# Output and down projections with one 512-column matmul over the high and low inputs

## The reference, cut to what matters

```python
def conv_ffn(h, w_in, conv_w, conv_b, w_out):
    z = h @ w_in
    u, g = z[..., :D_FF], z[..., D_FF:]
    a = causal_dwconv(u, conv_w) + conv_b
    return (jax.nn.silu(a) * g) @ w_out

h = h + even_mixer(hn, ...)          # ends in  concat(y_a, y_b) @ w_out
h = h + conv_ffn(rmsnorm(h, g), ...)
h = h + odd_mixer(hn, ...)           # ends in  y @ w_out
```

## Time and profile before

| | us |
|---|---|
| median of 3 runs | 996.73 (994.44 to 996.92) |
| span of the profiled execution | 994.4 (its own time outside the span is not given; the lowest run, 994.44, is the same within 0.1) |
| PE busy | 936.8 (94%) |
| PEld busy | 912.8 (92%) |
| DVE busy | 648.7 (65%) |
| ACT busy | 526.3 (53%) |
| POOL busy | 376.2 (38%) |
| mean granted TensorE clock | 0.976 |

### The profile page before, as it was taken

The page is one execution under the profiler, slowest core; times in us unless marked ns, Lnnn a source line. Parts: engine busy times, 40 slices in busy tenths (PEclk is TensorE's granted clock), DMA queues, the critical chain, the costliest instruction groups (busy, mean ns, idle before and its releaser), DMA issues.

```text
span 994.4 us, 20944 instructions
## 1 busy us (share of the span) xinstructions
PE 936.8 (94%) x7618; PEld 912.8 (92%) x7618; DVE 648.7 (65%) x1109; ACT 526.3 (53%) x847; POOL 376.2 (38%) x158
## 2 busy tenths in 40 slices
PE   8899999994699899999999999989999999999994
PEld 8789999994699899999999999979899999999993
DVE  6998766660454855576666564789747877765366
ACT  6346755550444455575555554545557766664353
POOL 3333434440442432234433433313322444343452
PEclk9899999998799999999999999989999999999997
DMA  7445666572643344456555654334333655565521
GB/s 259 158 148 174 206 201 199 188 232 75 200 166 107 132 151 135 136 173 213 185 172 195 226 184 154 107 127 139 117 121 133 201 188 182 173 228 186 179 80 43
DMA packets 46173, 163.37 MB, mean 164 GB/s; under 512 B 4985, under 2 KB 9593, under 8 KB 46123
## 3 DMA queue, kind: packets, MB, share of 16 engines
q1 hardware_dynamic: 41704, 158.19, 48.7%
q10 hardware_dynamic: 4419, 4.49, 1.3%
HBM read 161.58 MB, written 3.31 MB: 166 GB/s over the span
## 4 chain that ended last, share of the span: by engine, by line
PE 55%; issue 21%; DVE 12%; POOL 5%; ACT 3%; another core or an unknown queue 3%; DMA 1%; SPq 0%; POOLq 0%; ACTq 0%; DVEq 0%
PE psum L1239 17%; PE psum L1240 17%; PE psum L1241 17%; POOL wl L434 5%; DVE work L878 2%; DVE wl L781 1%; DVE h L1214 1%; ACT wh L479 1%; DMA raw<-in_even_in 1%; PE psum L1411 1%; ACT work L640 1%; PE psum L1380 1%; DVE work L1072 1%; PE psum L1388 1%
## 5 line engine op out<-in xcount | busy, mean ns | idle before, releaser
L434 POOL TENSOR_TENSOR wl<-raw,wh 128x1024 fp32r<-128x1024 f32 (+2 forms) x137 | 358.8, 2620 | 581.1 <-ACT wh L479 580.9
L1239 PE MATMUL psum<-xs,wh 128*128 128x256 f32 x1632 | 467.9, 287 | 4.3 <-DVE xs L797 2.1
L1240 PE MATMUL psum<-xs,wh 128*128 128x256 f32 x1632 | 463.2, 284 | 0.0
L1241 PE MATMUL psum<-xs,wl 128*128 128x256 f32 x1632 | 463.1, 284 | 0.0
L479 ACT ACTIVATE wh<-raw 128x1024 fp32r<-128x1024 f32 (+2 forms) x270 | 300.8, 1119 | 286.0 <-PE psum L1241 250.9
L1239 PEld LDWEIGHTS psum<-xs,wh 128*128 128x128 f32 x1632 | 314.5, 193 | 10.9 <-issue 4.0
L1240 PEld LDWEIGHTS psum<-xs,wh 128*128 128x128 f32 x1632 | 314.6, 193 | 0.2
L1241 PEld LDWEIGHTS psum<-xs,wl 128*128 128x128 f32 x1632 | 314.4, 193 | 0.0
L781 DVE TENSOR_TENSOR wl<-raw,wh 128x1024 fp32r<-128x1024 f32 (+1 forms) x133 | 183.8, 1382 | 125.1 <-ACT wh L479 125.0
L1239 PE MATMUL psum<-ys,wh 128*128 128x256 f32 x672 | 192.5, 286 | 22.1 <-DVE h L946 22.1
L1240 PE MATMUL psum<-ys,wh 128*128 128x256 f32 x672 | 191.3, 285 | 0.0
(11 more groups left out here) (195 smaller groups left out, 726.5 us busy)
## 6 DMA issues: line engine op xcount, KB each, us to landing
raw<-in_up SPq DMA_DIRECT2D x132, 512.0 KB, 4.1
raw<-in_down SPq DMA_DIRECT2D x48, 704.0 KB, 4.4
raw<-in_qkv SPq DMA_DIRECT2D x48, 512.0 KB, 3.3
raw<-in_even_in SPq DMA_DIRECT2D x16, 512.0 KB, 4.3
raw<-in_out SPq DMA_DIRECT2D x16, 512.0 KB, 3.4
raw<-in_ple SPq DMA_DIRECT2D x8, 640.0 KB, 3.8
raw<-in_even_out SPq DMA_DIRECT2D x8, 512.0 KB, 3.2
toeplitz_dram<-table_dram ACTq DMA_DIRECT2D x1, 2176.0 KB
```

Source lines behind the costliest of these rows:

```text
L434: nc.gpsimd.tensor_tensor(low, raw[:, s, 0:tiles * P], high.bitcast(f32), ALU.subtract)\
L1239: nc.tensor.matmul(bank, high_w[:, w], high, start=first, stop=False)
L1240: nc.tensor.matmul(bank, high_w[:, w], low, start=False, stop=False)
L1241: done = nc.tensor.matmul(bank, low_w[:, w], high, start=False, stop=last)
```

## The change

For the phases that read `ys`, `unit` gets `halves=True` and a whole bank of 512 columns. High weights meet the high and the low half of the input in one matmul of 512 columns: the first 256 columns of the bank get high by high, the last 256 high by low. Low weights by high input is still a matmul of 256 columns, into the second half. So two matmuls and two weight loads stand for a tile where three stood. The bank's two halves must then be summed: VectorE makes two adds into `h` in place of one (`add_halves`), the second behind a wait for the first (`steps`), and only the second signals `bank_read`. The phases that read `xs` (even_in, up, qkv, ple) stay as they are.

```diff
-        spare_bank = psum[:, 6:7, 0:SEQ]
+        spare_bank = psum[:, 6, :]
...
+            def add_halves(m, bank):
+
+                for half in range(2):
+                    part = bank.rearrange("p (c t) -> p c t", c=2)[:, half:half + 1, :]
+                    added = nc.vector.tensor_tensor(h[:, ds(m, 1), :], h[:, ds(m, 1), :], part, ALU.add)
+                    if half == 0:
+                        steps(added)
+                return added
...
-                        nc.vector.tensor_tensor(h[:, ds(m, 1), :], h[:, ds(m, 1), :], unit_bank(name, i, s), ALU.add)\
-                          .then_inc(bank_read, 1)
+                        add_halves(m, unit_bank(name, i, s)).then_inc(bank_read, 1)
...
-                        nc.vector.tensor_tensor(h[:, ds(m, 1), :], h[:, ds(m, 1), :], proj[:, c:c + 1, 0:SEQ], ALU.add)\
-                          .then_inc(bank_read, 2)
+                        add_halves(m, proj[:, c, :]).then_inc(bank_read, 2)
...
-            def unit(q, s, bank, inputs, tiles, start=True, stop=True, ready=None, read=None):
+            def unit(q, s, bank, inputs, tiles, start=True, stop=True, ready=None, read=None, halves=False):
...
-                    high, low = inputs(t)
                     first, last = start and n == 0, stop and n == len(tiles) - 1
                     w = slice(t * P, (t + 1) * P)
+                    if halves:
+                        nc.tensor.matmul(bank, high_w[:, w], inputs(t), start=first, stop=False)
+                        done = nc.tensor.matmul(bank[:, SEQ:2 * SEQ], low_w[:, w], inputs(t)[:, 0, :], start=False, stop=last)
+                        continue
+                    high, low = inputs(t)
                     nc.tensor.matmul(bank, high_w[:, w], high, start=first, stop=False)
                     nc.tensor.matmul(bank, high_w[:, w], low, start=False, stop=False)
                     done = nc.tensor.matmul(bank, low_w[:, w], high, start=False, stop=last)
...
+            def both_ys(t):
+                return ys[:, t, :, :]
...
             def out_rest(name):
-                each_quad(pe, 1, quads_of[name], quad_of(name, from_ys))
+                each_quad(pe, 1, quads_of[name], quad_of(name, both_ys, whole_bank, True))
...
-                        unit(q, s, slot_bank(c), lambda t: from_ys(b * HALF + t), range(HALF), start=b == 0, stop=b == 1,
-                             ready=ready, read=q * RING - 2 + 2 * c).then_inc(units_done, 1)
+                        unit(q, s, whole_bank(c), lambda t: both_ys(b * HALF + t), range(HALF), start=b == 0, stop=b == 1,
+                             ready=ready, read=q * RING - 2 + 2 * c, halves=True).then_inc(units_done, 1)
```

More of the change, by code:

```diff
@@ L332, in unit_bank @@
                 return spare_bank
-            return proj[:, s:s + 1, 0:SEQ]
+            return proj[:, s, :]
         def column(name, m):
@@ L933, in body @@
                             split_ahead(name, i, s)
-                phase(name, body)
+                phase(name, body, RING)
             def residual_down(name, n):
@@ L955, in body @@
                             split_ahead(name, i, 3)
-                phase(name, body)
+                phase(name, body, 2)
             def up(name, layer, chunks, both):
@@ L1248, in slot_read, with begin, whole_bank @@
                 return None if isinstance(q, int) and q == 0 else q * RING + s - 3
-            def begin(q, slots, bank, read, inputs, ready, late=1):
+            def begin(q, slots, bank, read, inputs, ready, late=1, halves=False):
                 for s in slots:
-                    unit(q, s, bank(s), inputs, range(DC - late), stop=False, ready=ready if s == slots[0] else None, read=read(s))
+                    unit(q, s, bank(s), inputs, range(DC - late), stop=False, ready=ready if s == slots[0] else None, read=read(s),
+                         halves=halves)
                 for s in slots:
-                    unit(q, s, bank(s), inputs, range(DC - late, DC), start=False, ready=ready if s == slots[0] else None)\
-                      .then_inc(units_done, 1)
+                    unit(q, s, bank(s), inputs, range(DC - late, DC), start=False, ready=ready if s == slots[0] else None,
+                         halves=halves).then_inc(units_done, 1)
             def slot_bank(s):
                 return proj[:, s, 0:SEQ]
+            def whole_bank(s):
+                return proj[:, s, :]
             def from_xs(t):
                 return xs[:, t, 0, :], xs[:, t, 1, :]
-            def from_ys(t):
-                return ys[:, t, 0, :], ys[:, t, 1, :]
+            def both_ys(t):
+                return ys[:, t, :, :]
             def statistics(n):
@@ L1273, in statistics, with quad_of @@
                 last.then_inc(stat_ready, 1)
-            def quad_of(name, inputs):
+            def quad_of(name, inputs, bank=slot_bank, halves=False):
                 def quad(i, slots=range(RING)):
@@ L1278, in quad @@
                     for s in slots:
-                        unit(q, s, slot_bank(s), inputs, ALL, read=slot_read(q, s)).then_inc(units_done, 1)
+                        unit(q, s, bank(s), inputs, ALL, read=slot_read(q, s), halves=halves).then_inc(units_done, 1)
                 return quad
@@ L1456, in out_unit @@
                     ready = (lambda t: pe.wait_ge(ys_ready, ys_base[f"att{layer}"] + t + 1)) if s == 0 else None
-                    return unit(out_q, s, unit_bank(out_name, 0, s)[:, 0, :], from_ys, tiles, ready=ready, read=out_q * RING, **flags)
+                    return unit(out_q, s, unit_bank(out_name, 0, s), both_ys, tiles, ready=ready, read=out_q * RING, halves=True, **flags)
                 last_pair = PAIRS - 1
@@ L1529, in _ @@
             q = base["even_out"]
-            begin(q, (0, 1), slot_bank, lambda s: slot_read(q, s), from_ys, lambda t: pe.wait_ge(ys_ready, t + 1), late=2)
-            quad_of("even_out", from_ys)(0, (2, 3))
+            begin(q, (0, 1), whole_bank, lambda s: slot_read(q, s), both_ys, lambda t: pe.wait_ge(ys_ready, t + 1), late=2,
+                  halves=True)
+            quad_of("even_out", both_ys, whole_bank, True)(0, (2, 3))
             out_rest("even_out")
```

## The result

Median of 4 runs 1004.76 us (1004.31 to 1006.37), beside 996.83 (994.44 to 997.97) for the kernel before: ratio 1.0087, 95% interval [1.0075, 1.01], slower by 7.9 us where 1.3 less was forecast, and outside the range. The profiled execution took 1004.64 us, its span is 1002.8 against 994.4, its mean clock 0.966 against 0.976. (The time of a run is 1.8 to 2.5 us above its span in the runs whose two numbers are both recorded; so the run with the span of 994.4 was not the lowest, as the table of the kernel before supposes, but one near its median.) In the changed kernel the merged matmul is line 1246, the low-weight one 1247, the adds 917, and the three matmuls over `xs` 1250 to 1252.

What follows compares the result with a forecast made beforehand. PE's matmul pitch was taken to bound the down projections, VectorE's chain the ends of out0 and out1. Tiles saving 7.6 us against 6.3 us of second-add costs gave -1.3 us, 995.4 us, range 991 to 1001.5.

Steps and rivals of the forecast that it cites:

- What bounds the kernel: PE's pitch inside down phases, waits for VectorE ending out0 and out1, a 22.13 us table DMA stall in down0.
- The tile: Changed tiles: 344 ns for 360 from a fixed extra per matmul; 476 counted tiles save 7.6 us.
- rival 2: Half the matmul's extra grows with columns: 512 at 232 ns, tile 352, sum +2.5 us, 999.2 us; 20%.
- The table DMA and the restart: End of even_out and down0: table DMA issued 1.7 us later, plus 0.45 us for the second add at restart.
- GpSimd's split as cover: Output projections: under a GpSimd split the low half ends about 0.28 us after it, so an added 0.45 us disappears.
- out0 and out1: Their VectorE chains lengthen by 2.25 us each; net cost 1.85 us at out0 and 2.15 us at out1.
- The clock: Ends of out0 and out1: PE idle about 1.2 and 2.6 us may bring 6.8 us at 1.2 GHz, costing 3.0 us.
- down2 into ple: Last chunk's low half has 0.55 us of slack against the added 0.45 us; cost 0.15 us at most.
- The sum: Whole kernel: tiles -7.6 us and costs 6.3 us give -1.3 us, 995.4 us against the median 996.73.
- rival 4: Slower by the clock behind out0 or out1: one 1.2 GHz stretch 998.4 us, 30%; two 1001.4 us, 12%.

Runs made afterwards that it cites:

- down_only: Changed kernel with the change kept in the three down projections alone, the output projections as before: 993.92 us, ratio 0.9968 to the kernel before.
- out_only: Changed kernel with the change kept in even_out, out0 and out1 alone, the down projections as before: 1005.5 us, ratio 1.0076 to the kernel before.
- late_wait: Kernel before, with ScalarE's wait for the table DMA and two bias loads moved behind down0: 973.1 us, ratio 0.9764.
- late_wait_down: Kernel before with the change in the down projections alone and ScalarE's wait for the table DMA moved behind down0: 967.77 us, ratio 0.9719.
- grouped_down: `down_only` with each unit's 512-column matmuls first and its 256-column ones behind them: 991.23 us, ratio 0.9948 to the kernel before.
- pitches: Kernel before with rows of fp32r and bf16 matmuls of several widths behind PE's last one, only to read pitches: 1034.71 us.
- pitches2: Changed kernel with rows of fp32r matmuls in mixed orders of width appended to PE's program, only to read pitches: 1046.99 us.
- keep_busy: Changed kernel with filler matmuls on spare data before PE's waits for tiles 5 and 6 of up1 and up2: 1001.39 us, ratio 1.0049 to kernel before.
- one_add: Changed kernel with only the first of the two adds, each bank's upper half left out of the sum: 994.07 us, ratio 0.9974 to the kernel before.
- two_adds_256: Changed kernel with three 256-column matmuls again, high by low into the upper half, both adds kept: 1007.11 us, ratio 1.011 to the kernel before.

## Why the prediction was wrong, step by step

Two steps failed. The term for the tiles (a tile costs 344 ns, -7.6 us) was mis-sized: 353.3 ns in two of three phases, -3.6 us. And the term for the clock stood at nothing in the sum, as a rival for which both falls together had 12%: the runs show +4.9 us.

- **What bounds the kernel: right.** PE's pitch inside the down projections, VectorE's chain at the ends of out0 and out1, the table DMA in down0. `down_only` and `out_only` split the change along that line, -2.9 and +8.7 us, though the two don't add up to the whole.
- **The tile: wrong in size.** The step was "a tile then costs 344 ns". It costs 353.3 in down1 and down2, by luck rival 2's number (352), for its reason doesn't hold: a 512 among its equals is 226.7, the rest comes with the alternation. Of the 9.3 ns too much, 2.7 are the fixed extra, 13.3 and not 10.4, and 6.6 the alternation, for which the prediction had no term. The stretch behind the stall in down0 has 346.7, but the half clock behind the restart lasts 5.7 us there where it lasted 5.0 before, which takes 0.3 us of that gain back. The 120 ns that I left for the 256 behind a 512 held (117 on average); the 512 was taken at 224 and is 236. Gained in the counted tiles: 1.29 + 1.17 + 1.17 = 3.6 us for 7.6.
- **The table DMA and the restart: right.** 1.83 us for 1.7; the restart came 2.53 later for 2.15. From the issue of the table DMA to that of the bias load that waits for it there are 154.9 us before and 155.1 after (up to 156.0 in the ten profiles in which ScalarE waits for it there), and that is most of the rest.
- **GpSimd's split as cover: right**, 0.47 us for a pair of chunks, and `wl`'s split sets the end of the low half. This is where a plain count of adds would have been wrong: it would give even_out and out0 3.6 us each.
- **out0 and out1: right.** The VectorE chain is 2.25 us longer, and PE's shorter tiles gave back 0.2. Out0 and the wait in up1 make +2.05 (-0.32 + 2.37) for 1.85, out1 and up2 +2.21 (0.22 + 1.99) for 2.15.
- **The clock: the mechanism was right, its chance was not.** I priced a fall at 3.0 us and gave two of them 12%. Both came, and up1 and up2 show 2.46 and 2.45. The price was for 6.8 us in full work; 5.66 of them were work at out0, and by the prediction's own factor that makes 5.66 x 93 / 213 = 2.5. As to the chance, I had weighed an idle of 2.62 with a fall against one of 2.20 without. My own forecast of the idle, 1.2 and 2.6, lay at the first of them and asked for more than 30 and 12%. The idle that came (0.78 and 2.36, 0.52 and 2.35) lies between the two rows, which then say nothing. And the row without a fall was one profile's luck: of the twelve others nine have the same wait of 2.20 to 2.22 us near 68 us, and each of the nine has a fall of 3.4 us behind it, in the unchanged kernel's own code too (`late_wait`). Shorter waits there went both ways: 1.75 and 1.76 (`late_wait_down`, `grouped_down`) without a fall, 1.84 (`pitches`) with one. That two falls of full length came is luck of this kind as well; `pitches2`, the same code, has one of half the length. The changed kernel, PE's stop and the clock behind it:

```profile
67.78 0.73 PE L1528 MATMUL psum<-work,qkv 128*128 128x256 f32 x2 [2.20 <-DVE work L887]
```

```profile
68.30:71.70 3.40, 3.40 (x12) 2.90 (x11) 3.22 (x7) 0.47 (x1) 0.00 (x0) 0.50 0.38 123
```

  `keep_busy` and `one_add` show that without the stop there is no fall: filled, or 1.52 to 1.64 long from start to start, it leaves the clock full. With the stop the fall came at seven of eight ends.
- **down2 into ple: wrong term, small.** +0.85 for 0.15. I looked at PE's slack for the last tile. The end of the kernel hangs on ScalarE's chain instead (last norm, square, table load, gates): from ple's first matmul to that table load it is 959.74 - 955.57 = 4.17 us, where it was 951.60 - 948.02 = 3.58 before, so 0.59. The other 0.3 lie behind VectorE's last operation, 3.8 us from the end for 3.4, and aren't the change's: `two_adds_256` has 3.4 there and `one_add` 3.8. The timelines of PE and ACT, first of the kernel before, then of the changed one:

```profile
948.02 0.28 PE L1555 MATMUL psum<-ps,wh 128*128 128x256 f32 x1
...
951.60 1.28 ACT L508 ACT_TABLE_LOAD   x1
```

```profile
955.57 0.28 PE L1571 MATMUL psum<-ps,wh 128*128 128x256 f32 x1
...
959.74 1.28 ACT L508 ACT_TABLE_LOAD   x1
```

- **The sum.** With the measured sizes it is -3.6 (tiles) + 2.5 (restart) + 2.0 + 2.2 (waits) + 0.9 (ple) + 4.9 (clock) = +8.9, less 0.5 for the attention, where 4.4 us of its fall were work for 5.7 before: the 8.4 of the span. The forecast missed 4.0 at the tile, 4.9 at the clock and 0.7 at ple. Rival 2 with two falls would have been 999.2 + 6.0 = 1005.2, beside the 1004.76. It stood nowhere, since I joined rival 2 with one fall only; that is how the range came to end at 1001.5. That end has a slip too: it adds 2.3 us for the one fall where rival 4 has 3.0, and the 10% for the pair is 20% of 42%, so 8. Neither would have brought 1004.76 into the range.

## What to carry to other kernels

A merge that saves instructions on one engine and adds one to another is worth what each phase's own bound says: do it where the matmul stream is the bound, leave it where a chain of dependent small operations is. When an added operation lengthens a wait of the matmul engine, read next to it the longest stop after which the clock stayed and the shortest after which it fell, in one measure and in more than one profile, since the same stop went both ways here. Then put the fall's price, times its chance, into the sum itself. Of two stalls in one profile the large one that neither busy engine makes is the better target: moving one wait gave 24 us where this change moved 3.

## What the runs showed of the hardware that I had not expected

- An fp32r matmul among equals costs its columns at 2.4 GHz plus 13.3 ns, at 256, 384 and 512 columns alike; in bf16 the extra is about 3.
- Alternating 512 and 256 columns costs 353.3 or 346.7 ns a pair, the one or the other over long stretches of one execution, and the same code has shown both. 384/256 pay nothing over their own pitches, 512/384 pay 14 ns a pair. Why isn't settled; what starts the one or the other rhythm wasn't tried.
- Two stops of PE, 0.62 to 1.06 and then 2.63 us from start to start, were followed by 6.8 us at 1.2 GHz in three places, by 3.4 in four and by none in one. A wait of 2.20 to 2.22 near 68 us was followed by 3.4 us in nine profiles of ten. Single stops of 1.52 and 1.64 were followed by none.
- What a fall costs goes with the part of it that falls on work: 5.7 of 6.8 us cost 2.45, and in the attention 3.9 to 6.7 us of work at the half clock made 1.2 us of difference between profiles.
- VectorE's low half ended 0.28 to 0.29 us behind GpSimd's split wherever they met, however much was put ahead of it, so that operations ahead of it are free up to the 1.2 us that it had waited.
